# Memory projections moved into the convolution stage, tokens picked on two halves of the matmul array, the scatter moved into the next expert's pass

## The reference

```python
# first block
xn = rms_norm(x, norm1_g);  h_in = xn @ w_in
attn = block_attention(q, k, v)                 # 8 heads
lru = (h_f + h_b) * gelu(lru_gate)              # two scans over the tokens
x = x + concat(rms_norm(attn), rms_norm(lru)) @ w_out
logits = xn @ w_router + b_router               # 32 experts, 4 for each token
g = xb @ w_gate[e];  u = xb @ w_up[e]
g = min(g, 7);  u = clip(u, -7, 7)
y = ((u + 1) * g * sigmoid(1.702 * g)) @ w_down[e]   # times the token's gate, summed over experts
# second block, two layers l
h = h + (mixer_ab, conv_module)[l](rmsnorm(h))
q = rmsnorm((hn @ wq[l]) per head)
k = rmsnorm((rmsnorm(mem, norm_mem[l]) @ wk[l]) per head)
v = rmsnorm(mem, norm_mem[l]) @ wv[l]
h = h + (softmax(q k^T / 16) v) @ wo[l]
h = h + (silu(xn @ w_gate) * (xn @ w_up)) @ w_down
```

## Time and profile before

| | before |
|---|---|
| median of 3 runs | 2231.03 us |
| profiled execution, its span | 2236.74 us, 2235.0 us |
| PE busy, share of the span | 2127.9 us, 95% |
| DVE busy | 553.5 us, 25% |
| ACT busy | 443.8 us, 20% |
| chain that ended last | PE 89%, DVE 5%, ACT 3%, issue 2% |
| weights read | 524 units of 1 MB |

### The profile page before, as it was taken

How to read it: one execution, slowest core, us unless ns; L and a number is a source line. 1 busy time by engine, 2 the same in 40 slices (tenths; PEclk the granted TensorE clock), 3 DMA queues, 4 the chain that set the end, 5 groups by cost and what they waited for, 6 DMA issues and landing times.

```text
span 2235.0 us, 27096 instructions
## 1 busy us (share of the span) xinstructions
PE 2127.9 (95%) x10318; PEld 1434.0 (64%) x10319; DVE 553.5 (25%) x1214; ACT 443.8 (20%) x793; POOL 6.9 (0%) x23
## 2 busy tenths in 40 slices
PE   8999989999999999999999899899999997999999
PEld 7686734444445444444444477587888886878888
DVE  4442211111111111111111147422000197121000
ACT  4332112222212221122212212222000114220000
POOL 0000000000000000000000000000000000000000
PEclk9999999999999999999999989899999998999999
DMA  8332679999989997999999932333444440424420
GB/s 324 127 118 95 247 288 422 422 422 422 422 361 354 421 422 308 388 422 422 422 422 422 421 122 95 132 132 132 151 151 151 151 151 8 143 79 149 154 90 19
DMA packets 78590, 564.36 MB, mean 253 GB/s; under 512 B 8864, under 2 KB 9248, under 8 KB 10176
## 3 DMA queue, kind: packets, MB, share of 16 engines
q1 hardware_dynamic: 77328, 554.94, 62.3%
q0 software_dynamic: 1200, 8.52, 0.9%
HBM read 558.19 MB, written 5.24 MB: 252 GB/s over the span
## 4 chain that ended last, share of the span: by engine, by line
PE 89%; DVE 5%; ACT 3%; issue 2%; DMA 0%; DVEq 0%; SPq 0%; ACTq 0%
PE bank L415 31%; PE bank L709 19%; PE bank L726 9%; PE bank L988 7%; PE bank L684 5%; DVE B L1917 3%; PE bank L736 3%; PE bank L758 2%; PE bank L550 2%; ACT B L1037 2%; PE bank L777 1%; PE bank L696 1%; PE bank L675 1%; PE bank L938 1%; PE bank L886 1%
## 5 line engine op out<-in xcount | busy, mean ns | idle before, releaser
L415 PE MATMUL bank<-xn,ring 128*128 128x256 f32 x2272 | 498.2, 380 | 4.6 <-DVE xn L1435 4.6
L415 PEld LDWEIGHTS bank<-xn,ring 128*128 128x128 f32 x2272 | 432.9, 191 | 66.9 <-issue 9.4
L709 PE MATMUL bank<-ring,B 128*64 128x512 f32 x1920 | 421.3, 597 | 7.8 <-issue 7.8
L1037 ACT ACTIVATE B<-bank 128x512 f32<-128x512 f32 (+3 forms) x283 | 144.0, 531 | 1238.3 <-PE bank L415 429.4
L709 PEld LDWEIGHTS bank<-ring,B 128*64 128x64 f32 x1920 | 136.1, 138 | 270.4 <-issue 267.1
L726 PE MATMUL bank<-ring,B 128*64 128x512 f32 x960 | 212.6, 595 | 0.0
L988 PE MATMUL bank<-B,ring 128*128 128x256 f32 x704 | 155.2, 379 | 0.0
L726 PEld LDWEIGHTS bank<-ring,B 128*64 128x64 f32 x960 | 66.3, 137 | 123.5 <-issue 119.9
L988 PEld LDWEIGHTS bank<-B,ring 128*128 128x128 f32 x704 | 134.0, 190 | 17.9
L1711 DVE TENSOR_TENSOR B<-bank,mbias 128x512 f32<-128x512 f32 x34 | 23.5, 692 | 428.6 <-PE bank L696 428.6
L684 PE MATMUL bank<-B 128*128 128x128 f32 x1056 | 125.2, 278 | 0.0
(11 more groups left out here) (294 smaller groups left out, 1501.6 us busy)
## 6 DMA issues: line engine op xcount, KB each, us to landing
ring<-in_stream SPq DMA_DIRECT2D x524, 1024.0 KB, 10.0
mem_kv<-ring POOLq DMA_DIRECT2D x4, 1024.0 KB, 7.1
B<-mem_kv POOLq DMA_DIRECT2D x4, 1024.0 KB, 6.8
xT<-in_x SPq DMA_DIRECT2D x1, 1024.0 KB, 4.9
ring<-in_mem SPq DMA_DIRECT2D x1, 1024.0 KB, 17.6
out_y<-xT SPq DMA_DIRECT2D x4, 256.0 KB, 2.3
tab<-in_tables SPq DMA_DIRECT2D x1, 960.0 KB, 10.7
tab<-in_tables SPq DMA_DIRECT2D x1, 544.0 KB, 11.6
```

The lines of the kernel that those rows point to most:

```text
L415: mm = pe.matmul(dst[:, m, :], tile(u, m * C + k), rhs[:, k, :], start=(k == 0), stop=(k == C - 1))
L709: mm = pe.matmul(PS[4 + kind][NARROW * h:NARROW * (h + 1), :], xs[:, k, NARROW * h:NARROW * (h + 1)], ring[:, expert_slot(j), D * kk + 512 ...
L1037: return act.activation(out_, in_, fn, **kw)
```

## The change

Four things are changed.

1. The keys and values of layer 1 (ck1, cv1: 8 units) are computed in the convolution stage instead of at the start. The normalized memory for them is written to xg at head 5, spilled to HBM, and read back after conv_in has begun. The spills of keys and values of layer 1 go. EARLY falls from 24 to 16. Two quarters of values(0) and the keys of layer 0 are the fills of heads 0 to 4; heads 5 to 7 have none; the last key unit comes behind the heads.
2. DVE convolves seven chunks instead of six, TensorE one.
3. In the experts, the next tokens are picked with the selection stationary (64 columns, two halves of the array side by side, 512 moving columns), copied, and turned by four transposes. In a wide pass there is a second such round. The scatter of an expert's output is split in two and put behind the turns of the next expert's pass. The selection without gates (sel) is signalled before that with gates (selg).
4. ACT takes a sigmoid of one element at the start of each pass.

```diff
-PLAN = [..., ("cv0", 4), ("ck0", 4),
-        ("ck1", 4), ("cv1", 4), ("w_out", 4), ("moe", 12 * E),
+        ("w_out", 4), ("moe", 12 * E),
...
-        ("conv_in", 8), ("conv_out", 4),
+        ("conv_in", 8), ("ck1", 4), ("cv1", 4), ("conv_out", 4),
...
-        ON_PE = (6, 7)
+        ON_PE = (7,)
...
+            def memory_fill(a):
+                if a < 2:
+                    pe.wait_ge(S["cv_ready"], a + 1)
+                    values(0, a + 2, a)
+                elif a < 5:
+                    memory_key(a - 2)
...
-            heads(0, 8, score1, output1, memory_keys, key_sums)
-            pe.wait_ge(S["ck_raw"], 8)
-            values(1, 0, 0)
+            heads(0, 8, score1, output1, memory_fill, fill_sum)
+            memory_key(3)
+            pe.wait_ge(S["o_ready"], 8)
+            key_sums(0, 3, 4, T)
...
-            for i, bank in ((1, 2), (2, 5), (3, 7)):
-                values(1, i, bank)
-            output_linear(AT["w_out"], xn)
+            output_linear(AT["w_out"], xn, None, spread_keys)
...
-            def gather(n):
+            def pick_tokens(n, w):
                 pe.wait_ge(M["sel_ready"], n + 1)
-                for c in range(C):
-                    for tk in range(2):
-                        mm = pe.matmul(PS[4 + c // 4][:, (c % 4) * WIDE:(c % 4 + 1) * WIDE],
-                                       xtok[:, tk, c * P:(c + 1) * P], sel[:, tk, :], ...)
+                for tk in range(2):
+                    for h in range(2):
+                        at = 512 * (h ^ w)
+                        mm = pe.matmul(PS[4][NARROW * h:NARROW * (h + 1), :],
+                                       sel[:, tk, NARROW * h:NARROW * (h + 1)], xtok[:, tk, at:at + 512], ...)
+                mm.then_inc(M["xa_mm"], 1)
+
+            def turn_tokens(n, w):
+                pe.wait_ge(M["xgt_ready"], nth(n, w))
+                for c in range(4):
+                    mm = pe.transpose(PS[5][:, c * P:(c + 1) * P], xgt[:, c * P:(c + 1) * P], tb("ident"))
...
                 turn(n, 0, 0)
-                pe.wait_ge(M["selT_ready"], n + 1)
+                scatter_halves(n, 0)
                 turn(n, 0, 1)
-                gather(n + 1)
-                pe.wait_ge(M["h_ready"], n + 1)
+                pick_tokens(n + 1, 0)
+                scatter_halves(n, 1)
+                turn_tokens(n + 1, 0)
+                pe.wait_ge(M["h_ready"], nth(n, 0))
...
                 mm.then_inc(M["y_mm"], 1)
-                pe.wait_ge(M["y_ready"], n + 1)
-                for c in (0, 4, 1, 5, 2, 6, 3, 7): (the scatter)
-                select_T(n + 1)
+                select_T(n, True)
...
             def wide_pass(n, e, frees):
+                pick_tokens(n, 1)
+                pe.wait_ge(M["y_ready"], n + 1)
+                pe.wait_ge(M["selT_ready"], n + 1)
+                scatter_halves(n, 0)
+                scatter_halves(n, 1)
+                turn_tokens(n, 1)
+                pe.wait_ge(M["xs_ready"], nth(n, 1))
...
+            pe.wait_ge(S["mem_back"], 32)
+            for j in range(4):
+                if j >= 2:
+                    pe.wait_ge(S["ck_raw"], 4 + j - 1)
+                stationary(AT["ck1"] + j, two(2 + j % 2), xg)
+                if j:
+                    key_sums(1, j - 1, 5, 2 * j - 2)
+            key_sums(1, 3, 5, 6)
...
             (behind layernorm's first sums) values(1, 0, 6)
             (behind its second sums)
+            for i in range(1, 4):
+                if i >= 2:
+                    pe.wait_ge(S["cv_ready"], 4 + i - 1)
+                values(1, i, 6 + i % 2)
-            output_linear(AT["conv_out"], yc, (S["yc_ready"], 0, 1))
+            output_linear(AT["conv_out"], yc, (S["yc_ready"], 0, 1), spread_keys_again)
...
             def act_pass(n, wide):
-                selected(n)
-                halves(n, 0)
+                f(small[:, 24:25], V("eps6"), ACT.Sigmoid)
...
-            for first in (0, 2, 4):
+            for group in ((0, 1), (2, 3), (4, 5, 6)):
                 for t in range(TAPS):
```

More of the change, by code:

```diff
@@ L451, in first_unit, with output_linear @@
                 stationary(u, dst, xg, gained(n), {(0, 7): lambda: stat(n), (1, 6): lambda: spread(n)})
-            def output_linear(first, rhs, ready=None):
+            def output_linear(first, rhs, ready=None, fill=None):
                 for j in range(4):
                     stationary(first + j, two(j), rhs, ready if j == 0 else None)
+                    if fill and j == 0:
+                        fill()
             def heads(first, count, score, output, fill=None, fill_sum=None):
@@ L697, in turn @@
                                       (gA, uA)[kind][w][:, c * P:(c + 1) * P], tb("ident"))
-                mm.then_inc(M[("tg_mm", "tu_mm")[kind] + ROUND[w]], 1)
+                mm.then_inc(M[("tg_mm", "tu_mm")[kind]], 1)
             def narrow_pass(n, e):
+                for name in ("xa_mm", "xs_mm"):
+                    pe.sem_inc(M[name], 1)
                 mm = None
@@ L751, in wide_pass @@
                         if w:
[L752 removed]
+                            pe.wait_ge(M[("g_ready", "u_ready")[kind]], nth(n, 0))
                         for j in range(4 * kind, 4 * kind + 4):
@@ L757, in wide_pass @@
                                 k = 2 * (j % 4) + kk
-                                mm = pe.matmul(PS[4 + kind][:, :], xs[:, k, :],
+                                mm = pe.matmul(PS[4 + kind][:, :], xw[:, k, :],
                                                ring[:, expert_slot(j), D * kk + 512 * w:D * kk + 512 * (w + 1)],
@@ L1019, in _ @@
             mm.then_inc(S["lnsum_mm"], 1)
+            values(1, 0, 6)
             for j in range(4):
@@ L1165, in key_chunks, with key_deviation @@
                 for c in range(2):
-                    last = f(kst[l][:, 2 * j + c, :], two(0)[:, c, :], ACT.Identity, scale=V(f"ckg{l}", c))
+                    last = f(kst[l][:, 2 * j + c, :], two(bank)[:, c, :], ACT.Identity, scale=V(f"ckg{l}", c))
                 last.then_inc(S["ck_raw"], 1)
-            def key_deviations(a):
-                chain.mark(f(ksum[:, 2 * a:2 * a + 2], PS[4 + a % 2][:, T:T + 2], ACT.Copy))
-                if a % 4 == 3:
+            def key_deviation(j, bank):
+                act.wait_ge(S["ksum_mm"], j + 1)
+                chain.mark(f(ksum[:, 2 * j:2 * j + 2], PS[bank][:, T:T + 2], ACT.Copy))
+                if j == 3:
@@ L1172, in key_deviations, with memory_fill @@
                     chain.settle()
-                    part = ksum[:, 2 * a - 6:2 * a + 2]
-                    f(part, part, ACT.Sqrt, scale=1.0 / T, bias=V("eps6")).then_inc(S["kstd_ready"], 1)
-            for i in range(4):
-                copy_values(0, i, i % 2)
+                    f(ksum[:, 0:8], ksum[:, 0:8], ACT.Sqrt, scale=1.0 / T, bias=V("eps6")).then_inc(S["kstd_ready"], 1)
+            def memory_fill(a):
+                if a < 2:
+                    copy_values(0, a + 2, a)
+                elif a < 5:
+                    key_chunk(0, a - 2, 0)
@@ L1178, in _, with fill_sum @@
+            def fill_sum(a):
+                if 2 <= a < 5:
+                    key_deviation(a - 2, 4 + a % 2)
+            for i in range(2):
+                copy_values(0, i, i)
             act.wait_ge(S["m_ready"], 1)
@@ L1382, in _ @@
                 f(sq[:, c, :], hc[:, c, :], ACT.Sigmoid, bias=V("ln_b", c)).then_inc(S["lnsig_ready"], 1)
+            for i in range(1, 4):
+                copy_values(1, i, 6 + i % 2)
             norm(6)
@@ L1686, in select, with weigh @@
                     if general:
-                        step.mark(o)
+                        last = o
                     else:
                         step.link(o)
-                        step.mark(stt(sel[:, tk, :], io, key2[:, tk, bass.ds(e, 1)], sel[:, tk, :],
-                                      ALU.is_equal, ALU.add))
+                        last = stt(sel[:, tk, :], io, key2[:, tk, bass.ds(e, 1)], sel[:, tk, :],
+                                   ALU.is_equal, ALU.add)
+                    if tk == 0:
+                        step.mark(last)
+                last.then_inc(M["sel_ready"], 1)
+            def weigh(n, e, step):
+                dve.wait_ge(M["sel_ready"], n + 1)
                 step.settle()
@@ L1745, in _ @@
                 select(0, 0, 0, False, first)
+                weigh(0, 0, first)
                 with dve.Fori(0, E) as e:
@@ L1907, in _ @@
             last = {}
-            for first in (0, 2, 4):
+            for group in ((0, 1), (2, 3), (4, 5, 6)):
                 for t in range(TAPS):
-                    for c in (first, first + 1):
+                    for c in group:
                         w = V("dw", c * TAPS + t)
```

299 lines of the change are left out of this document (172 added, 127 removed).

## The result

The changed kernel takes 2202.75 us in the median (2198.24 to 2205.45, 4 runs); the kernel before, on the same chip, 2230.97 (2228.8 to 2232.66, 4 runs). The ratio is 0.9872, with a 95% interval of 0.985 to 0.9894: faster by 1.3%. Repeated twice on other occasions it was 0.9859 and 0.9847, so 28 to 34.5 us. The forecast was 2195, range 2180 to 2216.

What follows compares the result with a forecast made beforehand. PE, busy 95% of the span, and in the experts also the equally full weight stream were taken as the bounds. Terms -50 - 21 + 35 = -36 took the profiled 2236.74 to 2200.7, less 5.7: 2195 us, range 2180 to 2216.

Steps and rivals of the forecast that it cites:

- Part 1: Start, up to the experts: moving layer 1's keys and values out saves 50 us, bounds -42 to -54.
- Rival C: Start: gives little more than the moved work costs, bare heads and tail 15 us more; 2210 us, chance 0.12.
- some 8 us of waiting come back: Start, up to w_out: PE sheds 61 us of work but w_out starts only 53.5 earlier.
- Part 2: Experts: shorter narrow passes limited by the weight stream's lead, longer wide passes, last scatter behind the loop; -21 us.
- the 2.3 by which the stream was to restart sooner: Experts behind the second wide pass: about 2.3 us of earlier stream restart, counted in the 11.5 saved there.
- Part 3: Convolution: moved key and value work, partly hidden by old waits and the chunk given to DVE, costs +35 us.
- The 5.7 that I took off for the profiled execution of before: Sum: the profiled execution was 5.7 us above the median, so 2200.7 became 2195.
- A: Experts give nothing: first passes lose their lead elsewhere, or waits at units cost the rest; 2216 us, chance 0.11.
- B: Experts: stream not the bound, its spacing an echo of PE's; experts give -48, total 2168 us, chance 0.05.
- D: Stream-paced expert passes: waits at units put the clock to 1.2 GHz, +128 us, 2323; with other losses chance 0.06.
- The prediction's two kinds of wait: PE's clock: 0.60 us waits in heads left it at 2.4 GHz; the 5.69 ahead of expert 1 brought 1.2 GHz.
- E: Experts: array halves don't run side by side, picking 3.5 instead of 1.75; 2198 us, inside the forecast's 0.66 chance.

Runs made afterwards that it cites:

- Half the stream: SyncE's loop over the ring loads only half of each unit (wrong weights): kernel after 2164.8 us, kernel before 2226.49 us, each in a single execution.
- the run on the last key unit: Kernel after with layer 0's last key unit moved behind the statistics, to run during the layernorm: 2189.36 us, ratio 0.9808.
- The two experiments on it: Kernel after with two convolution chunks on TensorE, six on DVE: 2208.3 us, ratio 0.9887; kernel after with gates sooner in DVE's taps: 2195.74 us, ratio 0.9835.

## Why the prediction was right, and where it was off

**What bounds the kernel.** Right in its main point: two engines at their limit in the experts. Half the stream gives the kernel before 3.7 us of loop, none of it in its usual pass, and the kernel after 31.

**Part 1, -50: measured -50.4.** The steps hold one by one: output of the heads, forecast 112.2, came at 112.36; the bare heads end at 153.57 (154.2), w_out starts at 175.86 (176.4), the experts at 233.97 (234). Rival C (15 less) is refuted. The part "some 8 us of waiting come back" is the 7.45 of the trace; moving one unit into that place got it back, as the run on the last key unit shows. It was priced well, and it was avoidable. Inside, two errors offset each other: the 2 us for the last key unit at the lower clock didn't come (7.07, full clock), and the statistics cost 5.41 where the chain had 1.7 for the second half of them.

**Part 2, -21: measured -14.4.** This is the term that was mis-sized, in three of its steps:

- The pass of PE's own is 27.3 us (27.2 forecast), the paced one 29.82 (29.8), five passes between the wide ones give 9.6 (10.2), the wide ones +5.7 each (+5.3). These are right.
- The passes up to the first wide one gave 14.2 (11.6 forecast). The forecast had kept the 5.69 ahead of expert 1, which went with the old code of the pass: expert 0 with that wait is 5.3 shorter. That is the wait and the 2.0 of the pass, less 2.35 for the clock in expert 0. Passes 1 to 11 then gave only 8.8, and 2.7 of them are expert 1 back at full clock. The likely reason is the stream: during the old wait it had filled the ring and all but stood still (DMA share 0.08), and this lead is missing now. No run tests that by itself.
- The passes behind the second wide one gave 8.65 (11.5 forecast). Their lead of 7.2 and the 1.8 behind the last paced unit came; the 2.3 by which the stream was to restart sooner didn't. Expert 31's eighth unit lands 355.7 us behind the end of the wide pass before and 356.0 after.
- The scatter behind the loop was priced at its 2.0 us. It cost 6.5: 2.0, a wait of 0.71 for DVE, 0.4 of slower matmuls, and the issue waits of the exit grew from 4.63 to 4.17 + 3.85. In the run with the experts' edits alone the same exit has 4.01 + 1.01, with half the stream 3.79 + 2.22; I did not settle what sets the second one, only that 3.7 us of it need both parts of the change.

That rows showed issue waits of 4.6 and 5.7 us at the two ends of the loop, and that the change edits the code at both, should have been a bound of some 4 us either way in the sum. It wasn't in it. So the term of -21 kept an entry wait that went, counted 2.3 us of an earlier restart that didn't come, and took the exit's issue waits as fixed; 6.6 us too much in all.

**Part 3, +35: measured +34.6.** The wait of 4.4 was named, and the 4.45 that came took the clock down as well (15.34 for 13.62); DVE's taps end ahead of PE's sums; the conv_out's place, forecast 1923 on the old scale, is 1851.42 + 71.3 = 1922.7. The two experiments on it say that the seventh chunk on DVE is worth 9.3 us of the stage, and the order of the gates up to 6.

**The sum and the medians.** -50.4 - 14.4 + 34.6 = -30.2, against 28.2, 30.7 and 34.5 in the medians of three comparisons. The forecast -36 was met by the profiled pair only because mixer came out 6.5 us luckier in one than in the other. The 5.7 that I took off for the profiled execution of before is of the same kind: 3.7 of it are that stage's.

**Rivals.** A (2216) is refuted by the run with the experts' edits alone, -19.9. B (2168) is refuted as a forecast and about right as a price: without the scatter's 2.0 behind the loop it gave -50 for a stream that keeps up, and with half the stream in both kernels the loop lost 46. D (2323) is refuted: some 37 waits of 0.55 us at units (20.5 / 0.55), three a pass, left the granted clock at 1.00 from 240 to 1200. The prediction's two kinds of wait (0.60 harmless, 5.69 not) are not the whole of it, though. In the kernel before, the granted clock also fell to 0.50 from 184.9 to 188.3, behind a wait of 1.47, and this unit of keys took 8.76:

```profile
184.71 8.76 PE L415 MATMUL bank<-ring 128*128 128x256 f32 x32
```

In the second profile of that kernel the same unit behind the same wait takes 7.07. With the fall behind 0.78 and 0.56 at the statistics above, the length of one wait doesn't tell whether the clock falls, and the rows that the prediction went by couldn't exclude D.

E: the halves run side by side, picking takes 1.94 for 1.75 forecast.

The Trainium skill (TensorE: Matmul & The Clock Gate, "HAM oscillation") describes a kernel whose DMA waits between short bursts bring the clock down again and again, and in its example these waits last some 3 to 5 us. The loop here has gaps of 0.55 us, and doesn't show the effect; in the same trace the clock did stand at 0.50 behind waits of 7.45 and 4.45 us. That is no contradiction. The prediction took the rule for waits much shorter than those that the section tells of, and this is where its reading of the rule was wrong; D's 128 us were the prediction's own estimate.

## What to carry to other kernels

Where a stream runs at its full rate beside an engine that is nearly as busy, price a faster pass by the lead that is left at each point of the ring, and not by the pass: here edits worth 46 us of loop beside half the stream brought 18 beside the whole one. When work is moved out of a stage, look at what it covered there; one remaining unit of it put into the new gap gave 8 to 9 us. And compare stage by stage with a second execution: the part that nobody changed differed by 6.5 us.

## What the runs showed that I had not expected

- The wait of 5.6 us (5.69, 5.54, 5.64 in three executions) ahead of the second pass of the old loop is absent with the new pass, and is 3.05 when the stream carries half its bytes. That it is code fetched beside the stream would fit, but was not tested by itself.
- The first part of the unchanged stage takes 170.3 to 178.3 us in the fourteen profiled executions, and it goes with the granted clock there: 0.98 at 170.3, 0.95 at 174.6, 0.92 at 178.3.
